# A decoder trunk on one core: the compressed scores of the first head group in one matmul for both key parts, added up by ScalarE and VectorE

## The reference

```python
def nsa(nq, nkv, ngate, kpos, kw1, kb1, kw2, kb2, ...):
    kc = compress(kv[0], kpos, kw1, kb1, kw2, kb2)
    vc = compress(kv[1], vpos, vw1, vb1, vw2, vb2)
    ...
    def block(b):
        sc = jnp.einsum('bhgqd,bhcd->bhgqc', qb, kc)
        mc = (c_start + CMP_BLOCK - 1)[None, :] <= t[:, None]
        pc = masked_softmax(sc, mc)
        o_cmp = jnp.einsum('bhgqc,bhcd->bhgqd', pc.astype(vc.dtype), vc)
        ...
        return gb[..., 0:1] * o_cmp + gb[..., 1:2] * o_slc + gb[..., 2:3] * o_win

def conv_ffn(h, w_up, conv_w, conv_b, w_down):
    u = h @ w_up
    ...
    return (jax.nn.gelu(a) * v) @ w_down
```

## Time and profile before

| | |
|---|---|
| median of 3 runs | 1379.64 us (1379.24 to 1380.26) |
| the profiled execution's own time | 1378.21 us |
| its span in the trace | 1376.4 us |
| TensorE's granted clock | 0.999 of full speed |
| busy: TensorE, VectorE, ScalarE, GpSimd | 98%, 53%, 44%, 51% |
| the chain that ended last | TensorE 87%, ScalarE 5%, VectorE 4%, issue 2%, GpSimd 1% |

### The profile page before, as it was taken

One profiled execution on the slowest core, in us unless ns is written; L12 is line 12 of the kernel. 1 busy time (PEld: TensorE's weight loads), 2 busy tenths in 40 slices (PEclk: granted clock), 3 DMA queues, 4 the chain that ended last, 5 costly groups with the idle time before them and its releaser, 6 DMA issues.

```text
span 1376.4 us, 17693 instructions
## 1 busy us (share of the span) xinstructions
PE 1351.3 (98%) x6904; PEld 1113.3 (81%) x6904; DVE 725.5 (53%) x908; ACT 603.2 (44%) x1039; POOL 698.8 (51%) x544
## 2 busy tenths in 40 slices
PE   8999999999999999999999999999999999999998
PEld 5889876778888888888888888767798888888886
DVE  5506658745554544654463075677355554556443
ACT  5233577745433333423441336676463333334222
POOL 2544677744544444544465456776544444445441
PEclk9999999999999999999999999999999999999999
DMA  5433320031432333333233334101233333333331
GB/s 205 138 99 108 119 81 16 1 123 62 118 97 92 102 98 92 97 103 92 62 123 102 116 100 134 34 15 43 81 98 102 105 94 92 104 96 92 98 102 61
DMA packets 34883, 127.19 MB, mean 92 GB/s; under 512 B 3952, under 2 KB 4464, under 8 KB 34416
## 3 DMA queue, kind: packets, MB, share of 16 engines
q1 hardware_dynamic: 34656, 125.53, 29.5%
q10 hardware_dynamic: 144, 0.52, 0.1%
HBM read 123.94 MB, written 2.10 MB: 92 GB/s over the span
## 4 chain that ended last, share of the span: by engine, by line
PE 87%; ACT 5%; DVE 4%; issue 2%; POOL 1%; DMA 0%; DVEq 0%; POOLq 0%; ACTq 0%; SPq 0%
PE bank L1755 33%; PE bank L1408 17%; PE bank L1787 17%; PE bank L1424 5%; PE bank L1652 3%; PE bank L1690 2%; ACT E L825 1%; PE bank L1713 1%; PE bank L1512 1%; PE bank L1714 1%; DVE pt_l L945 1%; PE bank L1619 1%; PE bank L1598 1%; PE bank L1376 1%; DVE s_bias L1209 1%
## 5 line engine op out<-in xcount | busy, mean ns | idle before, releaser
L550 POOL TENSOR_TENSOR w_lo<-raw,w_hi 128x1024 fp32r<-128x1024 f32 x216 | 519.8, 2412 | 469.7 <-ACT w_hi L650 469.3
L650 ACT ACTIVATE w_hi<-raw 128x1024 fp32r<-128x1024 f32 x220 | 231.0, 1055 | 240.8 <-DMA raw<-wstream 240.5
L1755 PE MATMUL bank<-act_hi,w_hi 128*128 128x512 f32 (+1 forms) x768 | 286.0, 372 | 0.6 <-DVE act_lo L945 0.6
L1755 PE MATMUL bank<-act_hi,w_lo 128*128 128x512 f32 (+1 forms) x768 | 285.2, 371 | 0.0
L1755 PE MATMUL bank<-act_lo,w_hi 128*128 128x512 f32 (+1 forms) x768 | 285.2, 371 | 0.0
L904 ACT ACTIVATE cv<-bank,par 128x512 f32<-128x512 f32 x88 | 68.4, 778 | 286.0 <-PE bank L1755 286.0
L1337 DVE SCALAR_TENSOR_TENSOR cv<-bank,par,cv 128x511 f32<-128x511 f32 x88 | 66.0, 749 | 225.2 <-ACT cv L904 225.2
L1755 PEld LDWEIGHTS bank<-act_hi,w_hi 128*128 128x128 f32 x768 | 144.6, 188 | 26.9 <-DVE act_lo L945 1.6
L1755 PEld LDWEIGHTS bank<-act_lo,w_hi 128*128 128x128 f32 x768 | 144.7, 188 | 25.0
L1755 PEld LDWEIGHTS bank<-act_hi,w_lo 128*128 128x128 f32 x768 | 144.6, 188 | 24.8
L1408 PE MATMUL bank<-w_hi,act_hi 128*128 128x512 f32 (+1 forms) x384 | 144.5, 376 | 0.6 <-DVE w_lo L945 0.5
(11 more groups left out here) (178 smaller groups left out, 2195.2 us busy)
## 6 DMA issues: line engine op xcount, KB each, us to landing
raw<-wstream SPq DMA_DIRECT2D x220, 512.0 KB, 3.6
g_all<-gains SPq DMA_DIRECT2D x2, 2048.0 KB, 7.2
x_out<-x SPq DMA_DIRECT2D x8, 256.0 KB, 2.0
x<-x_in SPq DMA_DIRECT2D x3, 512.0 KB, 9.1
const<-consts SPq DMA_DIRECT2D x1, 1030.0 KB, 13.7
x<-x_in SPq DMA_DIRECT2D x2, 256.0 KB, 5.2
g_all<-gains ACTq DMA_DIRECT2D x1, 512.0 KB, 5.1
par<-pars SPq DMA_DIRECT2D x2, 235.0 KB, 3.6
```

Of the source, the lines that this page charges most:

```text
L550: nc.gpsimd.tensor_tensor(w_lo[:, s, :], raw_slot(s), r32(w_hi[:, s, :]), ALU.subtract)\
L650: nc.scalar.activation(w_hi[:, s, :], raw_slot(s), ACT.Copy).then_inc(hi_ready, 1)
L1755: last = mm(bank[:, b, first:end], a, v, start=(k == 0 and n == 0), stop=(k == KD - 1 and n == 2), skip_group_check=True)
```

## The change

The high and the low part of the keys now stand side by side in one tensor `Kc` (partition, group, part, 32 keys). For group 0 one matmul of 64 columns takes both parts, so that the product with the high part and the product with the low part land in neighbouring blocks of 32 PSUM columns and are no longer added up by TensorE. They need two banks (6 and 7, of which only 7 was used), with a mask of 256 columns for each. ScalarE copies the 512 columns of the high products to `cE` in SBUF behind exponential 13, and VectorE adds the 512 columns of the low products to it behind minimum 14. `compressed_first(0)` moves from behind job 13 to round 1 and works from `cE` in SBUF; the exponential and the four steps behind it move by one round, and so do `queries_first(6)` and `queries_rest(6)`. Bank 6 was first written in `product(0)`, behind the retention's last use of it (`y_step`); that wait moves ahead of the scores, and `product(0)` and feature tile 7 wait for VectorE's addition. Group 1 computes as before, with the keys from `Kc`.

```diff
-        KcH = sb("KcH", [P, NKV * NCP], F32R)
-        KcL = sb("KcL", [P, NKV * NCP], F32R)
+        Kc = sb("Kc", [P, NKV, 2, NCP], F32R)
...
-        CMP_BANK, CMP_AT = (7, 0), (0, 24)
+        CMP_AT = (1, 24)
-        Q6_END, Q7_END = 1, 7
+        Q6_END, Q7_END = 2, 7
...
+                    if z == 13:
+                        act.wait_ge(cs_done, upto(cs_done, l, 1))
+                        nc.scalar.activation(cE[:, 0].rearrange("p (b r) c -> p b r c", b=2),
+                                             bank[:, 6:8, :].rearrange("p b (r s c) -> p b r s c", s=2, c=NCP)
+                                             [:, :, :, 0, :], ACT.Copy).then_inc(c_high, 1)
...
+                def compressed_added():
+                    rows = cE[:, 0]
+                    parts = bank[:, 6:8, :].rearrange("p b (r s c) -> p b r s c", s=2, c=NCP)
+                    dve.wait_ge(c_high, upto(c_high, l, 1))
+                    nc.vector.tensor_tensor(rows.rearrange("p (b r) c -> p b r c", b=2),
+                                            rows.rearrange("p (b r) c -> p b r c", b=2), parts[:, :, :, 1, :],
+                                            ALU.add).then_inc(c_added, 1)
+
                 def compressed_first(g):
-                    at, b = 7 * g, CMP_BANK[g]
-                    rows = bank[:, b, :].rearrange("p (r c) -> p r c", c=NCP)
+                    at = 7 * g
                     stat = c_stat[:, g * 16:g * 16 + 16]
-                    dve.wait_ge(cs_done, upto(cs_done, l, g + 1))
+                    if g:
+                        dve.wait_ge(cs_done, upto(cs_done, l, 2))
+                        rows = bank[:, 0, :].rearrange("p (r c) -> p r c", c=NCP)
+                    else:
+                        dve.wait_ge(c_added, upto(c_added, l, 1))
+                        rows = cE[:, 0]
...
-                    if z == 13:
-                        compressed_first(0)
+                    if z == 14:
+                        compressed_added()
...
-                    if k == CMP_AT[1]:
-                        compressed_first(1)
+                    if k in CMP_AT:
+                        compressed_first(CMP_AT.index(k))
...
+                def compressed_scores_0(t):
+                    if t == 0:
+                        pe.wait_ge(kc_l, upto(kc_l, l, 2))
+                        pe.wait_ge(k_l, upto(k_l, l, 8))
+                        pe.wait_ge(q_l, upto(q_l, l, 4))
+                        pe.wait_ge(y_step, upto(y_step, l, 8))
+                    if t % 2 == 0:
+                        mm(bank[:, 6 + t // 2, :].rearrange("p (t r s c) -> p t r s c", t=2, r=G, s=2)[:, :, :, 0, :],
+                           ident_b[:], mask[:, t:t + 2].unsqueeze(2).broadcast_to([P, 2, G, NCP]),
+                           start=True, stop=False, skip_group_check=True)
                     for r in range(G):
-                        at = (t * G + r) * NCP
-                        q = QS[:, G * g + r, t * P:(t + 1) * P]
-                        for m, key in enumerate((KcH, KcL)):
-                            last = mm(bank[:, b, at:at + NCP], q, key[:, g * NCP:(g + 1) * NCP],
+                        at = (t % 2 * G + r) * 2 * NCP
+                        last = mm(bank[:, 6 + t // 2, at:at + 2 * NCP], QS[:, r, t * P:(t + 1) * P],
+                                  Kc[:, 0].rearrange("p s c -> p (s c)"), start=False, stop=True, skip_group_check=True)
...
-                            pe.wait_ge(y_step, upto(y_step, l, 8))
+                            pe.wait_ge(c_added, upto(c_added, l, 1))
...
-                            pe.wait_ge(c_step, upto(c_step, l, 3))
+                            pe.wait_ge(c_added, upto(c_added, l, 1))
```

More of the change, by code:

```diff
@@ L288, in build @@
         cs_done = sem("cs_done", 2)
+        c_high = sem("c_high", 1)
+        c_added = sem("c_added", 1)
         c_step = sem("c_step", 14)
@@ L800, in compressed_keys @@
                     for half in range(2):
-                        nc.scalar.activation(KcH[half * DH:(half + 1) * DH, :], kcf[:], ACT.Copy).then_inc(kc_h, 1)
+                        nc.scalar.activation(Kc[half * DH:(half + 1) * DH, :, 0, :],
+                                             kcf[:].rearrange("p (g c) -> p g c", g=NKV), ACT.Copy).then_inc(kc_h, 1)
                 def compressed_values():
@@ L1194, in compressed_rests @@
                     for half in range(2):
-                        minus(KcL[half * DH:(half + 1) * DH, :], kcf[:], r32(KcH[0:DH, :])).then_inc(kc_l, 1)
+                        minus(Kc[half * DH:(half + 1) * DH, :, 1, :], kcf[:].rearrange("p (g c) -> p g c", g=NKV),
+                              r32(Kc[0:DH, :, 0, :])).then_inc(kc_l, 1)
                 def compressed_values_rest():
@@ L1601, in job_scores @@
                     last.then_inc(s_done, 1)
-                def compressed_scores(g, t):
-                    b = CMP_BANK[g]
+                mask = cmask_b[:].rearrange("p (t c) -> p t c", t=T)
+                def compressed_scores_0(t):
                     if t == 0:
@@ L1608, in compressed_scores, with compressed_scores_1 @@
                         pe.wait_ge(k_l, upto(k_l, l, 8))
[L1609 to L1613, removed]
+                        pe.wait_ge(q_l, upto(q_l, l, 4))
[4 more added lines that the diff above has]
+                           start=True, stop=False, skip_group_check=True)
+                    for r in range(G):
+                        at = (t % 2 * G + r) * 2 * NCP
+                        last = mm(bank[:, 6 + t // 2, at:at + 2 * NCP], QS[:, r, t * P:(t + 1) * P],
+                                  Kc[:, 0].rearrange("p s c -> p (s c)"), start=False, stop=True, skip_group_check=True)
+                    if t == T - 1:
+                        last.then_inc(cs_done, 1)
+                def compressed_scores_1(t):
+                    if t == 0:
+                        pe.wait_ge(q_l, upto(q_l, l, 8))
+                        pe.wait_ge(y_l, upto(y_l, l, 4))
+                        mm(bank[:, 0, :], ident_b[:], mask.unsqueeze(2).broadcast_to([P, T, G, NCP]),
                            start=True, stop=False, skip_group_check=True)
@@ L1616, in compressed_scores @@
                         at = (t * G + r) * NCP
-                        q = QS[:, G * g + r, t * P:(t + 1) * P]
-                        for m, key in enumerate((KcH, KcL)):
-                            last = mm(bank[:, b, at:at + NCP], q, key[:, g * NCP:(g + 1) * NCP],
+                        q = QS[:, G + r, t * P:(t + 1) * P]
+                        for m in range(2):
+                            last = mm(bank[:, 0, at:at + NCP], q, Kc[:, 1, m, :],
                                       start=False, stop=(m == 1), skip_group_check=True)
@@ L1670, in _ @@
                     if 11 <= n < 15:
-                        compressed_scores(0, n - 11)
+                        compressed_scores_0(n - 11)
                 def turn_p(k):
@@ L1723, in _ @@
                         if k == min(Q7_AT):
-                            pe.wait_ge(c_step, upto(c_step, l, 3))
+                            pe.wait_ge(c_added, upto(c_added, l, 1))
                         feature_tile(l, 7, range(*Q7_AT[k]))
                     if CMP_AT[1] - T <= k < CMP_AT[1]:
-                        compressed_scores(1, k - CMP_AT[1] + T)
+                        compressed_scores_1(k - CMP_AT[1] + T)
                     if k in Y_AT:
```

## The result

The changed kernel took 1385.34 us, the median of 5 runs (1384.85 to 1386.92), against 1379.64 us (1379.00 to 1380.55, 5 runs) on the same chip: 5.7 us more, a ratio of 1.0045 with a 95% interval of 1.0033 to 1.0056. The forecast was 1380.4, range 1377.0 to 1382.5. The first rows are from the page after: busy time, and the chain of waits by engine.

What follows compares the result with a forecast made beforehand. TensorE bounds until 215.74 us, then ScalarE and VectorE until 241.58. Per layer -1.77 matmuls, +0.03 masks, +0.64 addition wait, +1.33 subtraction and queue, +0.17 list: +0.4; two layers +0.8 on 1379.64 gives 1380.4 us, range 1377.0 to 1382.5.

Steps and rivals of the forecast that it cites:

- The list behind it: VectorE's and ScalarE's work behind the subtraction: from its end at 205.99, exponential 19 begins at 216.15, 0.4 us late.
- The subtraction in SBUF: `compressed_first(0)` behind `p_rest(1)`: the subtraction meets GpSimd's first `w_lo`, takes 2.4 us and ends at 205.99.
- X: The start of exponential 15, forecast at 200.25 in place of 201.70, from which the steps behind it are timed.
- One sign: Expected in the profile after: `turn_p(5)` waits for `pt_l`, starting at 209.92 in place of 209.69.
- the +0.8 of the forecast: Forecast loss over two layers, from +0.4 us per layer in the start of exponential 19.
- Rival (c): GpSimd's second `w_lo` also goes ahead of the waiting subtraction: 2.8 us per layer, +5.6, 1385.2 us; chance 0.05.
- Rival (a): The subtraction isn't held, taking 0.68 to 0.85 us: exponential 19 0.44 us early, -0.9, 1378.7 us; chance 0.28.
- VectorE's list decides alone: With the subtraction not held, VectorE's 6.9 us plus about 0.5 held by ScalarE's `p_round(6)` puts exponential 19 at 215.3.
- The upper value of 4.8 us for the subtraction: Upper end of the subtraction's time if GpSimd's second `w_lo` went first as well; 2.4 us was taken.

Runs made afterwards that it cites:

- e5: Changed kernel with group 0's bound as a small reduction in place of a tensor-scalar, one more memset per layer; 1380.64 us, ratio 1.0007 to before.
- e1: Changed kernel with group 0's bound and subtraction fused into one instruction at the same place; 1381.40 us, ratio 1.0008 to before.
- e7: Changed kernel with only GpSimd's second `w_lo` moved to its round 8, the first left in place; 1380.66 us, ratio 1.0007 to before.
- e2: Changed kernel with both of GpSimd's `w_lo` of the output projection moved to its round 8; 1377.51 us, ratio 0.9985 to before.
- e3: Changed kernel with `compressed_first(0)` directly behind minimum 15, ahead of the two `p_rest`; 1377.47 us, ratio 0.9986 to before.
- e4: Changed kernel with `compressed_first(0)` behind minimum 15, and exponential, four steps and tile 6 queries back in their rounds before the change; 1377.59 us, ratio 0.9981.
- e8: Changed kernel with bound and subtraction fused, directly behind minimum 15, and following steps back in their rounds before the change; 1378.15 us, ratio 0.9989.

## Why the prediction was wrong

Right were these steps, by the trace after:

- Matmuls of 64 columns cost 0.11 us each: the timeline has two of them start at 195.01 and 195.12. The chain has "PE bank L1638 x4" at 0.36 to 0.37 us where it had 0.80 for eight, so four fewer save 0.43 us; the forecast had named 0.4 to 0.45 for the four. Job 14 starts at 197.85 (forecast 197.86).
- The addition takes 0.68 us (0.69), and feature tile 7 starts at 199.74 (199.81), 1.17 us early instead of 1.10. The copy is hidden.
- Exponential 15 at 200.18 (200.25), `w_lo` 2.83 us behind it (2.8), the subtraction's own time under one hold 2.43 in e5 (2.4).
- The list behind it: from the subtraction's end to exponential 19 the forecast had 216.15 - 205.99 = 10.16 us; e1, e5 and e7 have 10.10, 10.10 and 10.11.

The step that failed is "The subtraction in SBUF". It let the bound through at 0.2 us ("the bound at X + 3.1, the subtraction at X + 3.3") and made the subtraction meet the first `w_lo`. But the bound had begun 0.28 us into that `w_lo` and was itself held: 2.13 us. The subtraction then met the second `w_lo`: 2.79. It ended at 208.25, not 205.99: 2.26 us per layer. The fallen clock, of which the forecast had nothing, adds 0.54. Together 2.80, less 0.06 by which the list was shorter: 2.74, and that is 218.89 - 216.15. One sign changed with it: the wait came at `turn_p(4)`, and `turn_p(5)` did not wait, as it does in e1 (0.90 us), where one hold is left. Over two layers it is 5.5 us, which with the +0.8 of the forecast makes the 6.3 of the trace.

Rival (c) had this time (1385.2) with a chance of 0.05, and not this mechanism. That its time came out so close is in part luck. It let one subtraction lose against both `w_lo`, and argued rightly from the earlier trace rows that a waiting instruction gets in between: e1 and e5 show it does, with GpSimd's pair lengthened to 5.17. What no rival had is two instructions of VectorE, each held once. What fits the rows is that GpSimd's second `w_lo`, already queued, started in the 0.04 us between the bound and the subtraction, for the pair is not lengthened (4.70). No run varies that gap.

Rival (a) had the condition of e2 and e3, nothing held, and was too cautious: it put exponential 19 at 215.3, 0.44 us early, since "VectorE's list decides alone". They have it 1.30 and 1.27 early. So the price of the list holds behind a hold, and not without one, where TensorE is last.

The trace before held a warning that was not used: VectorE's step of 16 elements in round 3, beside the second of GpSimd's pair, which ran to 209.28.

```profile
208.47 0.84 DVE L1287 SCALAR_TENSOR_TENSOR c_rec<-c_rec,gate_inv 128x16 f32<-128x16 f32 x1
```

It took 0.84 us, against 0.17 for the same instruction with nothing beside it (212.21 in e7), and ended 0.03 behind GpSimd. So here too a small instruction paid the whole rest of a large one. The forecast had read the pair's effect only from instructions of 512 columns.

The Trainium skill, "SBUF — State Buffer", section "SBUF: two separate sides", names two kinds of VectorE instruction that the lock with GpSimd concerns: those with two SBUF inputs, which the prediction used, and those in a 2-port mode, which it passed over. The Trainium skill, "VectorE: DVE Perf Modes", section "Mode 2×_2P — use both read ports for one tensor", puts a float32 tensor-scalar with source and result in SBUF there. By both the bound had to be held, and the runs agree: 2.13 us as a tensor-scalar, 0.19 as a reduction.

The range erred with the step: its upper end of 1382.5 left room for 1.4 us a layer over before, and the second hold alone costs 2.26. The upper value of 4.8 us for the subtraction was named in the working and then left out of the range on the strength of one row.

## What to carry to other kernels

When an operand moves from PSUM to SBUF, go through every VectorE instruction in the group, the smallest too, and ask of each whether it can be held by what GpSimd runs at that time; its price here was the rest of GpSimd's instruction, not a share of its own length. Two such instructions in a row beside two of GpSimd's pay twice. Put them ahead of GpSimd's work, or that work behind them, and the gain of the matmuls arrives: here 2.2 us in place of a loss of 5.7. Fusing them removes one of two holds and no more: e1 is still 1.6 us slower than before.

## What the runs showed of the hardware that was not expected

- A tensor-scalar of 16 elements took 2.13 us beside a GpSimd subtraction, a reduction of 32 elements at the same place 0.19.
- Behind a wait of TensorE of 2.59 us the granted clock was 0.50 from 209.3 to 212.7 us (0.54 from 891.7 to 895.2 in the second layer), and none of the kernels with waits of 0.9 us there showed it. The length of the wait does not settle it alone: at 218.8 to 223.5 us every kernel ends a wait of 1.6 to 1.7 us. Behind it the clock stayed at 1.00 in before, e2 and e4 (220 to 225 us), and fell in e3 (0.50) and e8 (0.66). The profiled execution of e3 took 1381.81 us where the median of its runs is 1377.47, so one profiled execution can be 4 us from the median. The stretch is in its trace:

```profile
220.00:225.00 5.00, 5.00 (x21) 4.19 (x20) 3.61 (x6) 1.14 (x3) 3.67 (x7) 0.50 0.00 0
```

- What stays open: why e8, with the same distance as e4, is no faster, and by its median 0.6 us slower (on the other chip, and the intervals overlap); and by what rule a waiting VectorE instruction goes ahead of GpSimd's next one, beyond the cases seen here.
